# dt's softplus on GpSimd, with its transpose, sums and broadcast placed earlier in the first group

## The chip, the cores and the metric

The kernel runs on one core of a Trainium2 chip. The metric is the device time of one execution in microseconds (us). The core has five engines that work side by side, each through its own list of instructions in order: TensorE (PE: matrix products and transposes, results into eight PSUM banks), VectorE (DVE) and ScalarE (ACT) for elementwise work, GpSimd (POOL), and SyncE (SP), which here only issues DMA transfers. Engines wait for each other through semaphores; an instruction that waits holds up everything behind it on its engine.

## The reference

A two-layer decoder trunk on 256 tokens of width 2048: a Mamba-2 layer, then sliding-window attention, each followed by a squared-ReLU MLP. The change lies in the Mamba-2 layer, in what it does with the step width dt (64 heads):

```python
zxbcdt = h @ w_in
z, xbc, dt_raw = ...                     # 4096, 6144 and 64 columns
xbc = silu(causal_conv(xbc) + conv_b)    # gives xs, Bm, Cm
dt = softplus(dt_raw + dt_bias)
A = -exp(A_log)
# per chunk of 128 tokens
xdt = xs * dt
cs = cumsum(dt * A)
decay = exp(where(causal, cs_i - cs_j, -inf))
y_intra = (C B^T * decay) @ xdt
y_inter = (C @ state) * exp(cs)
new_state = ...  exp(cs_last - cs) ...
```

The first thing that needs the broadcast rows of cs is the decay matrix of head group 0.

## The kernel before

All weights are read once, in chunks of 512 KB (128 x 1024 floats), through a ring of four raw buffers. For each chunk ACT makes a rounded high part `whi` (L820) and DVE the remainder `wlo` (L1258), into rings of eight slots. PE multiplies both. The function `step()` on ACT and on DVE handles one chunk; the order of the steps among the other work is written out by hand on each engine.

The first layer's input product goes by eight head groups. A group takes **row tiles** (`row_tile`: 128 output columns of B, C or xs for 256 tokens, two chunks each, 16 products at L451 and 16 at L457) and then a **column block**, the z block (`column_block`: 512 columns of z, eight chunks of 12 products at L476 to L478). The first group has one row tile more, the third, whose last 64 columns are dt. So its order on PE is: B, C, dt, four xs tiles, z block. Chunks are numbered c0, c1, ... in the order in which PE uses them: the fourth row tile (the first of xs) is c6 and c7, the fifth c8 and c9, and the z block of the first group is c14 to c21.

The row tiles use PSUM banks 0 and 1 in turn. Of each xs, B or C tile, ACT copies the cross product out (`cross`, L895), DVE adds it and frees the bank (`conv_sum`, L1381), makes the convolution (`conv`, L1391, L1395 twice, L1398), ACT the tanh (L905), DVE the silu product (L1403). The scan of group g is done in group g+1: PE transposes xs (`s1`), ACT makes the decay matrices of both chunks (`decay`, L922 and L926) from `csb`, the broadcast of the rows of cs, and DVE and PE go on from there.

What becomes of dt, step by step, with its engine:

- DVE adds the dt tile (`dt_add`, L1326) to `dth`; PE turns it into token order (`dt_transposes`, L528, bank 5).
- DVE adds the bias (L1334) and makes -|v| (L1339); ACT takes the exponential u (`dt_exp`, L875); DVE takes log(1+u) as a series in s = u/(u+2) (`softplus`, L1341 to L1361: the sum, the reciprocal, and 13 more), and writes `dt` and -dt*exp(A_log), `dv[11]`.
- PE sums `dv[11]` over the tokens by a triangular matrix (`dt_sums`, L571, L575, banks 4 and 5); DVE copies the result to `cs` (L1367); ACT takes two exponentials (`dt_decays`, L879, L881).
- PE turns cs (`cs_transposes`, L582); ACT copies it out (`dt_cs2`, L885, L887); POOL writes it to memory (L1997), copies the group's columns (L1962) and reads the rows back as a broadcast to all partitions, 1 MB, `csb` (L1963).

## Time and profile before

| | |
|---|---|
| median of 3 runs | 2385.54 us (2384.42 to 2387.88) |
| span of the profiled execution, first to last instruction | 2384.6 us |
| PE busy | 2368.3 us, 99% of the span |
| DVE busy | 1576.7 us, 66% |
| ACT busy | 1168.9 us, 49% |
| POOL busy | 42.7 us, 2% |
| chain that ended last | PE 94%, DVE 2%, DMA 1%, ACT 1%, issue 1% |

The profiled execution is known by its span; it lies 0.94 us below the median, inside the runs shown. PE busy at 99% says that only work added to PE, idle time of PE, or a lower clock of PE can move the end. The chain of work that ended last says where PE was not the one that everything waited for.

### The profile page before, as it was taken

The page shows a single profiled execution, that of the slowest core. Times are in us where ns is not written, and L with a number is a line of the kernel's source. Part 1 is how long each engine was busy: PE and PEld are TensorE (multiplying, and loading weights), DVE is VectorE, ACT ScalarE, POOL GpSimd, SP SyncE. Part 2 cuts the span into 40 slices and gives each one's busy share as a digit, 9 for nine tenths or more (in the row PEclk, how much of TensorE's full clock was granted, in tenths as well). Part 3 has the DMA queues.
Part 4 walks back from the last instruction along what each step waited for, and adds up shares of the span by engine and source line. Part 5 has one row for each costly group of instructions (what it writes and reads, how often), then busy time and mean ns, then how long its engine had stood idle before and what let it go on. Part 6 is the DMA issues. An engine that isn't in the chain of part 4 may idle for free.

```text
span 2384.6 us, 32345 instructions
## 1 busy us (share of the span) xinstructions
PE 2368.3 (99%) x12610; PEld 2001.0 (84%) x12610; DVE 1576.7 (66%) x2151; ACT 1168.9 (49%) x1742; POOL 42.7 (2%) x85
## 2 busy tenths in 40 slices
PE   9999999999999999999999999999999999999998
PEld 8888888888888888888888888778888888888886
DVE  7888888886568556556556577776864654655655
ACT  5555555564355444444345355774543443443441
POOL 0000000000000000000000000000000000000000
PEclk9999999999999999999999999999999999999999
DMA  8766666657657666666666646346776666666663
GB/s 234 222 198 191 191 188 192 193 163 243 193 181 229 218 187 188 198 186 193 195 187 188 200 157 204 117 132 200 200 234 187 190 196 183 194 199 187 191 195 109
DMA packets 487829, 455.10 MB, mean 191 GB/s; under 512 B 13792, under 2 KB 360080, under 8 KB 485392
## 3 DMA queue, kind: packets, MB, share of 16 engines
q1 hardware_dynamic: 484608, 433.51, 61.1%
q0 software_dynamic: 3088, 19.79, 2.4%
q8 instruction: 88, 1.44, 0.2%
q14 instruction: 45, 0.37, 0.0%
HBM read 450.55 MB, written 2.16 MB: 190 GB/s over the span
## 4 chain that ended last, share of the span: by engine, by line
PE 94%; DVE 2%; DMA 1%; ACT 1%; issue 1%; POOL 0%; SPq 0%; DVEq 0%; ACTq 0%
PE ps L451 25%; PE ps L476 16%; PE ps L477 15%; PE ps L478 15%; PE ps L457 13%; PE ps L509 2%; PE ps L507 2%; PE ps L508 2%; PE ps L528 1%; DVE wlo L1258 1%; PE ps L600 1%; ACT whi L820 0%; ACT pb L1178 0%; PE ps L714 0%; DMA csb<-cs_rows 0%
## 5 line engine op out<-in xcount | busy, mean ns | idle before, releaser
L1258 DVE TENSOR_TENSOR wlo<-raw,whi 128x1024 fp32r<-128x1024 f32 x817 | 994.9, 1223 | 678.2 <-ACT whi L820 677.3
L820 ACT ACTIVATE whi<-raw 128x1024 fp32r<-128x1024 f32 x817 | 860.0, 1057 | 848.8 <-PE ps L478 457.3
L451 PE MATMUL ps<-actA,whi 128*128 128x512 f32 x2704 | 650.0, 392 | 2.8 <-DVE xpad L1381 2.3
L451 PEld LDWEIGHTS ps<-actA,whi 128*128 128x128 f32 x2704 | 498.2, 189 | 101.4 <-DVE xpad L1381 2.5
L476 PE MATMUL ps<-whi,actB 128*128 128x512 f32 x1056 | 412.8, 391 | 0.0
L477 PE MATMUL ps<-wlo,actB 128*128 128x512 f32 x1056 | 411.0, 389 | 0.0
L478 PE MATMUL ps<-whi,actB 128*128 128x512 f32 x1056 | 410.9, 389 | 0.0
L457 PEld LDWEIGHTS ps<-actA,wlo 128*128 128x128 f32 x2704 | 347.2, 191 | 13.5
L457 PE MATMUL ps<-actA,wlo 128*128 128x256 f32 x2704 | 351.3, 283 | 0.0
L476 PEld LDWEIGHTS ps<-whi,actB 128*128 128x128 f32 x1056 | 198.2, 188 | 42.9 <-issue 1.3
L478 PEld LDWEIGHTS ps<-whi,actB 128*128 128x128 f32 x1056 | 198.2, 188 | 41.4
L477 PEld LDWEIGHTS ps<-wlo,actB 128*128 128x128 f32 x1056 | 198.3, 188 | 40.3
L476 PE MATMUL ps<-whi,actA 128*128 128x512 f32 x544 | 215.9, 397 | 0.0
L477 PE MATMUL ps<-wlo,actA 128*128 128x512 f32 x544 | 212.0, 390 | 0.0
L478 PE MATMUL ps<-whi,actA 128*128 128x512 f32 x544 | 212.0, 390 | 0.0
L476 PEld LDWEIGHTS ps<-whi,actA 128*128 128x128 f32 x544 | 102.2, 188 | 22.5 <-issue 1.3
L478 PEld LDWEIGHTS ps<-whi,actA 128*128 128x128 f32 x544 | 102.1, 188 | 21.6
L477 PEld LDWEIGHTS ps<-wlo,actA 128*128 128x128 f32 x544 | 102.3, 188 | 19.7
L834 ACT ACTIVATE actB<-fsq 128x256 fp32r<-128x256 f32 x120 | 50.2, 419 | 110.6 <-DVE fsq L1740 110.6
L1589 DVE TENSOR_TENSOR res<-ps,res 128x512 f32<-128x512 f32 x80 | 51.9, 686 | 62.6 <-PE ps L509 32.6
L905 ACT ACTIVATE thb<-xh 128x256 f32<-128x256 f32 x48 | 19.8, 413 | 115.2 <-DVE xh L1398 115.2
L1740 DVE SCALAR_TENSOR_TENSOR fsq<-fb 128x256 f32<-128x256 f32 x120 | 51.0, 425 | 4.1
(209 smaller groups left out, 1683.9 us busy)
## 6 DMA issues: line engine op xcount, KB each, us to landing
raw<-in_mlp_w SPq DMA_DIRECT2D x512, 512.0 KB, 4.5
raw<-in_a_w_in SPq DMA_DIRECT2D x162, 512.0 KB, 4.5
raw<-in_a_w_out SPq DMA_DIRECT2D x64, 512.0 KB, 4.7
raw<-in_b_w_q SPq DMA_DIRECT2D x32, 512.0 KB, 4.9
raw<-in_b_w_o SPq DMA_DIRECT2D x32, 512.0 KB, 4.0
csb<-cs_rows POOLq DMA_DIRECT2D x8, 1024.0 KB, 7.1
raw<-in_kv_w SPq DMA_DIRECT2D x16, 512.0 KB, 4.2
gb<-in_ln_g POOLq DMA_DIRECT2D x4, 1024.0 KB, 7.0
```

The lines of the kernel that those rows point to most:

```text
L451: e.matmul(ps[:, b, :], whi[:, s, k * P:(k + 1) * P], act[:, kt, :, :].rearrange("p a n -> p (a n)"), start=(kt == 0), stop=False)
L457: last = e.matmul(ps[:, b, T:2 * T], wlo[:, slots[half], k * P:(k + 1) * P], act[:, kt, 0, :], start=False, stop=(kt == KT - 1))
L476: e.matmul(ps[:, b0 + h, :], act[:, kt, 0, tk], whi[:, s, w], start=(kt == 0), stop=False)
L477: e.matmul(ps[:, b0 + h, :], act[:, kt, 0, tk], wlo[:, s, w], start=False, stop=False)
L478: last = e.matmul(ps[:, b0 + h, :], act[:, kt, 1, tk], whi[:, s, w], start=False, stop=(kt == KT - 1))
L507: e.matmul(ps[:, b0 + h, :], act[:, kt, 0, tk], hi_w, start=(kt == 0), stop=False)
L508: e.matmul(ps[:, b0 + h, :], act[:, kt, 0, tk], lo_w, start=False, stop=False)
L820: e.activation(whi[:, s, :], raw[:, r, :], ACT.Copy).then_inc(w_hi_done, C.up(w_hi_done))
L834: e.activation(dst, src, ACT.Copy).then_inc(act_hi_done, C.up(act_hi_done))
L1258: e.tensor_tensor(wlo[:, s, :], raw[:, r, :], whi[:, s, :].bitcast(F32), ALU.subtract).then_inc(w_split, C.up(w_split))
L1589: ins = e.tensor_tensor(r, ps[:, b, :], r, ALU.add)
L1740: e.scalar_tensor_tensor(fsq[:, i % 2, :], fb[:, i % 2, :], 0.0, fb[:, i % 2, :], ALU.max, ALU.mult).then_inc(f_squared, C.up(f_squared))
```

## The change

The diff, without the renamed arithmetic that stays the same:

```diff
@@ tensor, first_group
                 for i in range(4):
                     row_tile(i % 2, actA, lo_last=i > 0)
-                column_block(2, actA, after={0: [dt_transposes], 4: [dt_sums], 6: [cs_transposes]})
+                    if i == 0:
+                        dt_transposes()
+                column_block(2, actA, after={0: [dt_sums], 2: [cs_transposes]})
@@ scalar, first_group
                 constants_out()
                 cross(3, 10)
+                dt_exp()
                 step()
...
-                dt_exp()
-                for _ in range(4):
-                    step()
                 C.n[full[4]] += 1
                 dt_decays()
                 step()
-                step()
-                step()
                 dt_cs2()
-                step()
+                for _ in range(7):
+                    step()
@@ vector
-            def softplus():
+            def dt_in():
...
+            def dt_reciprocal():
                 e.wait_ge(uexp_ready, C.next(uexp_ready))
                 e.tensor_scalar(den_, u, 2.0, None, ALU.add).then_inc(dve_step, C.up(dve_step))
                 e.wait_ge(dve_step, C.now(dve_step))
-                e.reciprocal(rec, den_).then_inc(dve_step, C.up(dve_step))
...
+                e.reciprocal(rec, den_).then_inc(rec_ready, C.up(rec_ready))
@@ vector, first_group
                 conv(2, 0)
                 step()
                 step()
+                dt_in()
                 silu(2, 0)
                 conv(3, 0)
+                dt_reciprocal()
                 step()
                 step()
...
                 silu(5, 0)
-                step()
-                step()
-                softplus()
-                step()
-                step()
                 dt_sums()
+                step()
+                step()
                 rotations_out()
-                for _ in range(6):
+                for _ in range(8):
                     step()
@@ gpsimd
+            def softplus():
+                e.wait_ge(rec_ready, C.next(rec_ready))
+                e.tensor_tensor(s_, u, rec, ALU.mult).then_inc(pool_step, C.up(pool_step))
+                e.wait_ge(pool_step, C.now(pool_step))
+                e.tensor_tensor(s2_, s_, s_, ALU.mult).then_inc(pool_step, C.up(pool_step))
+                e.wait_ge(pool_step, C.now(pool_step))
+                e.tensor_scalar(q_, s2_, 1.0 / 15, None, ALU.mult).then_inc(pool_step, C.up(pool_step))
+                e.wait_ge(pool_step, C.now(pool_step))
+                for k in (13, 11, 9, 7, 5, 3):
+                    e.tensor_scalar(q_, q_, 1.0 / k, None, ALU.add).then_inc(pool_step, C.up(pool_step))
+                    e.wait_ge(pool_step, C.now(pool_step))
+                    e.tensor_tensor(q_, q_, s2_, ALU.mult).then_inc(pool_step, C.up(pool_step))
+                    e.wait_ge(pool_step, C.now(pool_step))
+                e.tensor_scalar(v, v, 0.0, None, ALU.max)
+                e.tensor_scalar(q_, q_, 1.0, 2.0, ALU.add, ALU.mult).then_inc(pool_step, C.up(pool_step))
+                e.wait_ge(pool_step, C.now(pool_step))
+                e.tensor_tensor(lp, q_, s_, ALU.mult).then_inc(pool_step, C.up(pool_step))
+                e.wait_ge(pool_step, C.now(pool_step))
+                dtf = dt[:, :, :].rearrange("p c h -> p (c h)")
+                e.tensor_tensor(dtf, v, lp, ALU.add).then_inc(pool_step, C.up(pool_step))
+                e.wait_ge(pool_step, C.now(pool_step))
+                e.tensor_scalar(q_, dtf, -1.0, None, ALU.mult).then_inc(pool_step, C.up(pool_step))
+                e.wait_ge(pool_step, C.now(pool_step))
+                e.tensor_tensor(dv[:, 11, :].rearrange("p (c h) -> p c h", c=NH), q_.rearrange("p (c h) -> p c h", c=NH),
+                                eA[:, :].unsqueeze(1).broadcast_to([P, NH, NHD]), ALU.mult).then_inc(dt_ready, C.up(dt_ready))
@@ gpsimd, main line
             for x, value in ((mhalf, -0.5), (per_gw, 1.0 / GW), (epsilon, EPS)):
                 e.memset(x, value)
+            softplus()
             e.wait_ge(cs_turned, C.next(cs_turned))
```

`dt_in` holds the bias and -|v|, as before. On GpSimd the fused two-step operations are split, so 13 operations of VectorE become 21 of GpSimd, each but one followed by a wait for the one before it. The counts of `step()` on each engine stay the same in sum.

On PE, where the first chunk of the first z block (c14) ends, the order before has dt's transposes:

```order
L478 MATMUL ps<-whi,actA 128x512
L528 MATMUL ps<-ident,dth 128x128 x2
L476 MATMUL ps<-whi,actA 128x512
L477 MATMUL ps<-wlo,actA 128x512
L478 MATMUL ps<-whi,actA 128x512
```

and the order after has the sums there (L571 and L575 of before are L572 and L576):

```order
L479 MATMUL ps<-whi,actA 128x512
L572 MATMUL ps<-dv,kst 128x64 x2
L576 MATMUL ps<-dv,kst 128x64
L477 MATMUL ps<-whi,actA 128x512
L478 MATMUL ps<-wlo,actA 128x512
```

The sums moved forward by four chunks of the z block, the transposes of dt out of it, behind the fourth row tile.

On DVE, from the convolution of the fifth row tile (the second of xs) to the products that remain before the cs copy, the order before has all of dt's arithmetic in one piece, behind the last silu and two chunks:

```order
L1403 SCALAR_TENSOR_TENSOR xT<-thb,xh 128x256
L1258 TENSOR_TENSOR wlo<-raw,whi 128x1024 x2
L1334 TENSOR_TENSOR dv<-ps,dtb 128x128
L1339 SCALAR_TENSOR_TENSOR dv<-dv 128x128
L1341 TENSOR_SCALAR dv<-dv 128x128
L1343 RECIPROCAL dv<-dv 128x128
...
L1361 SCALAR_TENSOR_TENSOR dv<-dt,eA 128x128
L1258 TENSOR_TENSOR wlo<-raw,whi 128x1024 x2
L1367 COPY cs<-ps 128x128
```

and the order after has its first four operations around the convolution of the fifth row tile:

```order
L1258 TENSOR_TENSOR wlo<-raw,whi 128x1024 x2
L1334 TENSOR_TENSOR dv<-ps,dtb 128x128
L1339 SCALAR_TENSOR_TENSOR dv<-dv 128x128
L1385 SCALAR_TENSOR_TENSOR xT<-thb,xh 128x256
L1363 TENSOR_TENSOR xpad<-ps,xpad 128x256
L1373 TENSOR_SCALAR xh<-xpad,cwg 128x256
L1377 SCALAR_TENSOR_TENSOR xh<-xpad,cwg,xh 128x256 x2
L1380 SCALAR_TENSOR_TENSOR xh<-xpad,cwg,xh 128x256
L1343 TENSOR_SCALAR dv<-dv 128x128
L1345 RECIPROCAL dv<-dv 128x128
L1258 TENSOR_TENSOR wlo<-raw,whi 128x1024 x2
```

Two operations moved ahead of that convolution and two behind it; the other 13 left DVE.

On POOL, behind the constants that it sets at the start, before:

```order
L1992 DMA Dsk<-in_a_D 128x64
L1995 MEMSET small 128x2 x3
L1997 DMA cs_rows<-cst 64x256
L1962 COPY csg<-cs 128x16
L1963 DMA csb<-cs_rows 128x2048
```

and after, where `dv` is dt's work space:

```order
L2003 MEMSET small 128x2 x3
L1967 ISA
L1967 TENSOR_TENSOR dv<-dv 128x128
L1969 TENSOR_TENSOR dv<-dv 128x128
L1971 TENSOR_SCALAR dv<-dv 128x128
...
L1986 TENSOR_SCALAR dv<-dt 128x128
L1988 TENSOR_TENSOR dv<-dv,eA 128x128
L2006 DMA cs_rows<-cst 64x256
```

The 21 operations stand ahead of the write of cs and of everything else that POOL does later.

## Rows read from the trace of the kernel before

**Rows 1.** Chain that ended last, 60 to 98 us: start us, us, what.
```profile
70.93 5.50 DMA raw<-in_a_w_in
...
77.58 0.28 ACT cst L885
...
82.55 8.51 DMA csb<-cs_rows
```

**Rows 2.** Timeline of PE, second group: start, us, engine, line, operation, [idle before <-releaser].
```profile
89.53 3.82 PE L451 MATMUL ps<-actA,whi 128*128 128x512 f32 x16
...
97.53 5.53 PE L451 MATMUL ps<-actA,whi 128*128 128x512 f32 x16 [2.28 <-DVE xpad L1381]
```

**Rows 3.** Timeline of PE, the same two row tiles of the third group.
```profile
154.36 3.82 PE L451 MATMUL ps<-actA,whi 128*128 128x512 f32 x16
...
159.93 3.82 PE L451 MATMUL ps<-actA,whi 128*128 128x512 f32 x16
```

**Rows 4.** Timeline of ACT, third group: its first decay.
```profile
148.67 2.45 ACT L922 ACTIVATE em<-csb,csg 128x128 f32<-128x128 f32 x8
```

**Rows 5.** Stretches: us, busy PE, PEld, DVE, ACT, POOL, PEclk, DMA share, GB/s.
```profile
97.50:100.00 2.50, 2.47 (x8) 1.95 (x9) 2.38 (x6) 2.47 (x6) 0.93 (x2) 0.69 0.62 171
...
102.00:103.00 1.00, 1.00 (x6) 0.82 (x5) 1.00 (x2) 1.00 (x2) 0.00 (x0) 1.00 1.01 385
```

**Rows 6.** Timeline of PE, first group: fifth row tile; dt's transposes, sums, cs transposes.
```profile
37.17 3.82 PE L451 MATMUL ps<-actA,whi 128*128 128x512 f32 x16
...
56.62 0.38 PE L528 MATMUL ps<-ident,dth 128*128 128x128 f32 x2
...
67.77 0.55 PE L571 MATMUL ps<-dv,kst 128*128 128x64 f32 x4
...
73.93 0.38 PE L582 MATMUL ps<-ident,cs 128*64 128x128 f32 x2
```

**Rows 7.** Timeline of DVE, first group, 33 to 63 us.
```profile
33.89 0.42 DVE L1326 TENSOR_TENSOR dth<-ps,dth 128x256 f32<-128x256 f32 x1
...
42.80 0.42 DVE L1403 SCALAR_TENSOR_TENSOR xT<-thb,xh 128x256 f32<-128x256 f32 x1
...
45.71 1.22 DVE L1258 TENSOR_TENSOR wlo<-raw,whi 128x1024 fp32r<-128x1024 f32 x1
...
51.28 1.22 DVE L1258 TENSOR_TENSOR wlo<-raw,whi 128x1024 fp32r<-128x1024 f32 x1
52.80 1.23 DVE L1258 TENSOR_TENSOR wlo<-raw,whi 128x1024 fp32r<-128x1024 f32 x1 [0.30 <-ACT whi L820]
...
61.89 0.95 DVE L1343 RECIPROCAL dv<-dv 128x128 f32<-128x128 f32 x1
62.88 0.29 DVE L1345 TENSOR_TENSOR dv<-dv 128x128 f32<-128x128 f32 x1
```

**Rows 8.** Timeline of POOL.
```profile
82.41 0.20 POOL L1962 COPY csg<-cs 128x16 f32<-128x16 f32 x1 [3.48 <-DMA cs_rows<-cst]
...
157.41 0.47 POOL L1962 COPY csg<-cs 128x16 f32<-128x16 f32 x1 [27.21 <-ACT em L922]
...
676.93 0.19 POOL L1977 TENSOR_TENSOR small<-small 128x1 f32<-128x1 f32 x1 [139.84 <-DVE small L1645]
677.19 0.57 POOL L1980 TENSOR_TENSOR small<-small 128x1 f32<-128x1 f32 x1
690.32 0.70 POOL L1977 TENSOR_TENSOR small<-small 128x1 f32<-128x1 f32 x1 [12.55 <-DVE small L1645]
691.09 1.43 POOL L1980 TENSOR_TENSOR small<-small 128x1 f32<-128x1 f32 x1
```

**Rows 9.** Timeline of DVE beside three of those operations.
```profile
156.82 1.01 DVE L1395 SCALAR_TENSOR_TENSOR xh<-xpad,cwg,xh 128x256 f32<-128x256 f32 x2
...
690.27 0.69 DVE L1270 TENSOR_TENSOR actA<-hf_early,actA 128x512 fp32r<-128x512 f32 x1
690.88 1.22 DVE L1258 TENSOR_TENSOR wlo<-raw,whi 128x1024 fp32r<-128x1024 f32 x1
```

More of the change, by code:

```diff
@@ L142, in build @@
     clamped = nc.alloc_semaphore("clamped")
+    rec_ready = nc.alloc_semaphore("rec_ready")
     nab_ready = nc.alloc_semaphore("nab_ready")
@@ L1328, in dt_add @@
                 e.memset(small[:, 95:96], 0.0).then_inc(dt_summed, C.up(dt_summed))
-            v, nab, u, den_, rec, s_, s2_, q_, lp = [dv[:, i, :] for i in range(9)]
-            def softplus():
+            v, nab, u, den_, rec = [dv[:, i, :] for i in range(5)]
+            def dt_in():
                 e.wait_ge(per_head_in, C.next(per_head_in, 3))
@@ L1501, in first_group @@
                 silu(5, 0)
+                dt_sums()
                 step()
                 step()
-                softplus()
-                step()
-                step()
-                dt_sums()
                 rotations_out()
-                for _ in range(6):
+                for _ in range(8):
                     step()
@@ L1981, in norm_rstd @@
                         rstd_ready, C.up(rstd_ready))
+            v, _, u, _, rec, s_, s2_, q_, lp = [dv[:, i, :] for i in range(9)]
+            def softplus():
[23 more added lines that the diff above has]
+                                eA[:, :].unsqueeze(1).broadcast_to([P, NH, NHD]), ALU.mult).then_inc(dt_ready, C.up(dt_ready))
             e.wait_ge(x_in[2], C.next(x_in[2]))
```

20 lines of the change are left out of this document (removed).

## The prediction, made before the changed kernel ran

> **What bounds the kernel now.** I read the page first: PE is busy for 99% of the span and 94% of the chain that ended last. So I looked for the places where that chain is not PE, and there is one of size behind the start: from 60 to 98 us it runs through dt. Its steps are the arithmetic of softplus, a load of weights (5.50 us from 70.93), ACT's copy of cs at 77.58, and the broadcast `csb`, 8.51 us from 82.55 [rows 1]. Behind it ACT makes the first decay and only then the weight chunk that DVE and PE want, and PE's fourth row tile of the second group starts 8.00 us after the third, with 2.28 us idle, released by DVE's convolution sum [rows 2]. In the third group the same two tiles are 5.57 us apart [rows 3].
>
> **What that place is worth.** The idle time with its restart costs 8.00 - 5.57 = 2.43 us. The 16 products behind it take 5.53 us, not 3.82: 1.71 more [rows 2, 3]. The stretches say why: the granted clock is 0.69 in the mean from 97.5 to 100, so part of it at 1.2 GHz, after PE had been idle, and full again (2.4 GHz) from 102 [rows 5]. Together 4.1 us, 0.17% of the span. If everything else were free, the change could bring this and no more, since no other wait hangs on dt.
>
> Does the new order remove it? Call T the time at which PE makes the sums. Before, T is 67.77, `csb` lands at 91.06, 23.3 later [rows 6, 1]. In that, ACT copied cs out 3.65 us after PE's transposes at 73.93 because chunks of weights stood ahead of the copy in ACT's order and one waited for its load [rows 6, 1]. The new order has one chunk between the exponentials and the copy, and the transposes still two chunks behind the sums: about 20 us from T to landing. In the third group, where nothing is late, the first decay starts 5.7 us ahead of the third tile [rows 3, 4]; for the second group that is 83.8. With T at 56.62 `csb` lands near 77, with a margin of 7 us, and when PE is held up at the sums both ends move with it. So the old wait goes, whatever else happens: -4.1.
>
> **The moved pieces, one by one.** dt's transposes on PE, now ahead of the fifth row tile at 37.17 [rows 6]: their input is ready at 34.5, 0.2 after `dt_add` ends at 34.31 [rows 7]. No wait; they cost PE the same 0.3 us here as there. `dt_in` on DVE goes between 42.80 and the silu: two operations of about 0.3 us, of which 0.2 falls into idle time ahead of the sum; the convolution ends 0.45 us later. ACT's exponential (0.3 us) is ready long before it is needed. The sum and the reciprocal stand behind the convolution: 45.71 + 0.45 + 0.26 + 0.95 = 47.4 for the end of the reciprocal [rows 7]. DVE and ACT now run about 1.2 to 1.6 us later through the last tiles. PE does not notice: c13, which DVE then finishes near 48.5 instead of 46.9, is used from 50.1, and each later chunk has more slack, 4 us and more in the z block. Chunks c18 and later now wait on DVE behind the copy of cs, which waits for the sums; PE takes c18 9 us after the sums, and DVE needs 2 us for it. No cost. The 13 operations that leave DVE (some 4.6 us from 62.88) were hidden; they bring nothing.
>
> **The piece that decides: 21 operations on POOL, and PE waits for the last.** PE reaches the sums after c14, at 56.62 [rows 6]. Until then POOL has 56.6 - 47.5 = 9.1 us, 0.43 us for each of 21. The trace shows no POOL operation of this shape. From below: one of 128x1 takes 0.19 us, and the next starts 0.26 after it; a copy of 16 columns takes 0.20 [rows 8]. At 0.26 the chain would take 5.5 us and PE would not wait. From above, undisturbed: DVE takes 0.29 for 128x128 [rows 7]; with the 0.07 for the semaphore 0.36, and twice DVE's time would be 0.65. I take 0.45, the floor of 0.26 with 0.15 to 0.2 for the 127 columns more: 9.5 us, ready at 57.0, a wait of 0.5.
>
> But POOL is not undisturbed. The same copy takes 0.20 us at 82.41 and 0.47 at 157.41, where it ends at 157.88, 0.05 after a DVE operation of two inputs from SBUF (157.34 to 157.83) [rows 8, 9]. The addition of one column takes 0.19 at 676.93 and 0.70 at 690.32: it ends at 691.02, and DVE's two-input subtraction beside it at 690.96. The next one takes 1.43 instead of 0.57: DVE's subtraction of 128x1024 ended at 692.10 [rows 8, 9]. So a POOL operation that starts while DVE reads two inputs from SBUF is held until that instruction ends, and then gets its turn. From 47.4 on DVE does little else: subtractions of 1.13 us, silu, three steps of each convolution. The Trainium skill, "SBUF — State Buffer", section "Who interferes with whom", says it as a rule: a VectorE instruction with two SBUF inputs and a GpSimd one that reads SBUF exclude each other for the whole instruction. By that rule too, the trace agrees (0.19 against 0.70).
>
> Counted in turns, with one POOL operation after each two-input DVE instruction and two in the 0.9 us of a sum and a one-input multiply between them: two subtractions and silu, 3 done by 50; the window, 5 by 51; three convolution steps, 8 by 52.6; subtractions of c15 and c16 and silu, 11 by 55.4; window, 13 by 56.4; convolution, 16 by 58; c17 and silu, 18 by 59.2. Then DVE itself stands at the cs copy, and the last 3 take 0.43 each: 60.5. DVE in turn is held by the POOL operations, some 0.07 us for each of 16: 61.6. PE waits from 56.6 to 61.6: **+5.0**. For the columns at nothing this count gives 59.3, +2.7; with 0.27 us and 0.2 us more for two and one input, 64.0, +7.4.
>
> The Trainium skill, "GPSIMD Engine Reference", section "3.1 Elementwise — side-by-side cycle accounting", gives 4497 ns for a two-input add of 2048 columns. An estimate from that page is 0.28 us for 128 columns, the upper end of what I counted; the wait would be about 6 us by it.
>
> After a wait of 2.28 us PE lost 1.71 to the clock [rows 2, 5]; I take +1.7 again, more for a longer wait being unseen.
>
> **Sum.** -4.1 + 5.0 + 1.7 = +2.6 us. Against the profiled span 2384.6 that is 2387.2; against the median of the runs, 0.94 higher, **2388.1**. With the ends of the wait, 2.7 and 7.4, it is +0.3 to +5.0, so 2385.8 to 2390.5. A measurement of this kernel can tell about 0.2%, 4.8 us: most of this counts as no change.
>
> **Rival A: POOL is fast enough.** The holding up costs little, because it applies to few instants or because POOL slips in between dependent DVE steps, and the chain takes its undisturbed 5.5 to 10 us. Then PE waits 0 to 1 us with no loss of clock, and the gain stays: -4.1 to -3.0, 2381.4 to 2382.5, still within 0.2%. For it: only tiny POOL operations were seen. Against it: each of the shown ones that met a two-input DVE instruction was held to its end. Chance 0.2.
>
> **Rival B: slower.** The same hold, but POOL loses the turn to a DVE instruction that is already queued, and advances only while DVE has no two-input one: in each row tile's 5.57 us the 0.9 us window and the 0.3 before the second subtraction [rows 7], 3 operations or so. Then 7 are done when DVE stops at the cs copy near 59, and 14 x 0.43 = 6.0 remain: ready at 65.0, PE waits 8.4, and with the clock and the gain +6.0: 2391.5. It decides from a wait of 7.2 us on, dt ready after 63.8. For it: several subtractions started 0.08 before the one ahead ended; against it: the addition at 690.32 did get its turn between two of them [rows 8, 9]. POOL operations dearer by 0.15 us than I took end here too. Chance 0.21.
>
> **Rival C: a first use costs.** POOL has not run a one-input multiply or add before this point, and a first use could cost time that the trace does not show; its first copy took the least of all, 0.20 [rows 8]. Each microsecond of it lengthens PE's wait by one; from 2.2 on the kernel is slower by over 0.2%, and with 3 (about seven undisturbed operations of 0.43) it would take 2391. The Trainium skill, "GPSIMD Engine Reference", "2.1 Instruction dispatch", gives some 6 us for the first call of a freshly loaded function, by which it would be 2394; no row here shows one. Chance 0.04.
>
> **Rival D: the change does not do what it says,** because `csb` stays last, through slower small transfers beside the weight loads. The margin of 7 us speaks against it. 2392. Chance 0.02.
>
> **How the numbers follow.** Forecast 0.53, rival A 0.2, B 0.21, C 0.04, D 0.02. Faster by more than 0.2% needs 4.8 us, over the 4.1 that are there: 0.03, out of A, for what I may have missed. Slower: B, C, D less what falls short of the bound, plus the end of the forecast: 0.28. The rest, 0.69, within. The range reaches from A's 2381.3 to B with a little more, 2392.5.
>
> **What the new profile would show.** PE: the 2.28 us ahead of the fourth row tile of the second group gone and its 16 products at 3.8 us; a new wait ahead of the sums in the first z block, released by POOL, of 3 to 7 us, and products behind it at a lower granted clock. POOL: 21 operations from 47.5 to about 61.5, some of 0.3 to 0.5 us and those beside DVE's subtractions of 1 us and more. DVE: idle ahead of the cs copy. `csb` on chip some 7 us before its use. I am wrong if POOL's operations don't end with DVE's two-input ones, if the chain takes under 9 us or over 17, or if PE waits elsewhere.

## The result, and the profile after

| | before | after |
|---|---|---|
| median, 10 runs each | 2385.54 us (2384.34 to 2389.33) | 2392.39 us (2391.92 to 2393.25) |
| ratio to before | | 1.0029 (95% interval 1.0021 to 1.0037) |
| span of the profiled execution | 2384.6 us | 2390.3 us |

The kernel is 0.29% slower. The forecast was 2388.1 with a range of 2381.3 to 2392.5: the time lies inside it, at its upper end, and outside the 0.2% that the forecast called no change. The spans differ by 5.7 us and the medians by 6.9; the readings below explain the 5.7.

**Where the time goes, in one table.** Two points of PE's timeline cut the stretch that the change touches: the start of the transposes of xs in the second group and the same in the third. In the profile they are the lines "ident,xT ... x8".

```profile
92.35 1.04 PE L529 MATMUL ps<-ident,xT 128*128 128x128 f32 x8
```

| start of that line | before | after | difference |
|---|---|---|---|
| second group | 82.44 | 92.35 | +9.91 |
| third group | 147.24 | 153.02 | +5.78 |
| between them | 64.80 | 60.67 | -4.13 |

So the first group lost 9.9 us, the second gave 4.13 back, and behind the third group's mark nothing more changes (5.78 against 5.7 in the spans). What the loss is made of, the list of PE's waits of after says (wait: us in total, times, longest):

```profile
PE ps L572 <- POOL dv L1988: 7.3, 1, 7.3
```

and PE's timeline, with the transposes of dt, the sums, and the third and fourth row tiles of the second group, which answer to [rows 2] (L452 is L451 of before, L572 is L571):

```profile
37.13 0.38 PE L529 MATMUL ps<-ident,dth 128*128 128x128 f32 x2
...
64.24 1.11 PE L572 MATMUL ps<-dv,kst 128*128 128x64 f32 x4 [7.26 <-POOL dv L1988]
...
99.46 3.82 PE L452 MATMUL ps<-actA,whi 128*128 128x512 f32 x16
...
105.02 3.82 PE L452 MATMUL ps<-actA,whi 128*128 128x512 f32 x16
```

PE waits 7.26 us at the sums. The old 2.28 us ahead of the fourth row tile of the second group are gone (the two tiles start 5.56 us apart, not 8.00), and its 16 products take 3.82 us instead of 5.53. The remaining 9.91 - 7.26 = 2.65 us is the clock. The stretches of after show it (columns as in [rows 5]: length, busy PE, PEld, DVE, ACT, POOL, granted clock, DMA share, GB/s):

```profile
56.00:60.00 4.00, 0.98 (x5) 0.48 (x3) 3.86 (x7) 1.65 (x3) 3.57 (x6) 0.90 0.70 224
60.00:64.00 4.00, 0.00 (x0) 0.00 (x0) 0.04 (x1) 0.66 (x1) 3.43 (x8) 0.50 0.44 131
64.00:68.00 4.00, 3.76 (x12) 3.28 (x13) 2.57 (x5) 1.31 (x3) 0.18 (x1) 0.50 0.02 4
68.00:72.00 4.00, 4.00 (x16) 3.21 (x15) 1.42 (x4) 0.00 (x0) 0.00 (x0) 0.82 0.93 253
```

The clock falls to 0.50 (1.2 GHz) while PE stands idle, and PE works on at that level until some way into the last stretch: 3.76 x 0.50 + 4.00 x 0.18 = 2.6 us of full-speed work lost. A mean of 0.82 over 4.00 us is 0.36 of them at 0.50, so PE works at the lower level for 3.76 + 1.44 = 5.2 us. Note the last columns too: from 64 to 68 us hardly any data moves (4 GB/s). That comes up again below.

**POOL**, the new chain, from its first to its last operation:

```profile
47.26 1.31 POOL L1967 TENSOR_TENSOR dv<-dv 128x128 f32<-128x128 f32 x1 [31.58 <-DVE dv L1345]
48.64 1.26 POOL L1969 TENSOR_TENSOR dv<-dv 128x128 f32<-128x128 f32 x1
49.99 0.59 POOL L1971 TENSOR_SCALAR dv<-dv 128x128 f32<-128x128 f32 x1
...
52.67 1.50 POOL L1976 TENSOR_TENSOR dv<-dv 128x128 f32<-128x128 f32 x1
54.26 1.50 POOL L1974 TENSOR_SCALAR dv<-dv 128x128 f32<-128x128 f32 x1
55.85 0.47 POOL L1976 TENSOR_TENSOR dv<-dv 128x128 f32<-128x128 f32 x1
56.40 0.58 POOL L1974 TENSOR_SCALAR dv<-dv 128x128 f32<-128x128 f32 x1
57.06 0.46 POOL L1976 TENSOR_TENSOR dv<-dv 128x128 f32<-128x128 f32 x1
...
58.27 1.50 POOL L1976 TENSOR_TENSOR dv<-dv 128x128 f32<-128x128 f32 x1
...
63.73 0.46 POOL L1988 TENSOR_TENSOR dv<-dv,eA 128x128 f32<-128x128 f32 x1
```

and DVE beside it:

```profile
47.09 2.56 DVE L1258 TENSOR_TENSOR wlo<-raw,whi 128x1024 fp32r<-128x1024 f32 x2
...
51.00 1.20 DVE L1377 SCALAR_TENSOR_TENSOR xh<-xpad,cwg,xh 128x256 f32<-128x256 f32 x2
...
52.63 1.22 DVE L1258 TENSOR_TENSOR wlo<-raw,whi 128x1024 fp32r<-128x1024 f32 x1
54.15 1.23 DVE L1258 TENSOR_TENSOR wlo<-raw,whi 128x1024 fp32r<-128x1024 f32 x1 [0.29 <-ACT whi L823]
...
58.23 1.22 DVE L1258 TENSOR_TENSOR wlo<-raw,whi 128x1024 fp32r<-128x1024 f32 x1
```

The chain runs from 47.26 to 64.19, 16.9 us. Five operations take 1.26 to 1.50 us, and each lies beside one of DVE's 128x1024 subtractions, ending some 0.3 us behind it (52.63 + 1.22 = 53.85, POOL 54.17). Of the other sixteen, fourteen take 0.45 to 0.47 (two inputs) and 0.53 to 0.59 (one input), beside DVE's 128x256 steps too (57.06, beside the convolution at 56.6 to 57.8). The two left are a one-input operation at 50.66, beside such steps, with 0.71 us, and the one at 61.65, which does not wait for the one ahead of it, with 0.30. From one start to the next these are about 0.55 and 0.66 us.

### The profile page after: what moved, and what is told of

It reads as the page before. It is cut to its first block, busy times and chain, and to the rows that moved or that the text cites. A ratio compares the mean times of both kernels' runs of the same rounds, so it can differ in the third digit from the quotient of the medians.

```text
span 2390.3 us, 32353 instructions
## 1 busy us (share of the span) xinstructions
PE 2368.6 (99%) x12610; PEld 2001.2 (84%) x12610; DVE 1573.1 (66%) x2138; ACT 1168.5 (49%) x1742; POOL 58.5 (2%) x106
## 3 DMA queue, kind: packets, MB, share of 16 engines
q8 instruction: 88, 1.44, 0.2%
## 4 chain that ended last, share of the span: by engine, by line
PE 95%; DVE 2%; ACT 1%; POOL 1%; issue 1%; DMA 0%; SPq 0%; DVEq 0%; ACTq 0%
PE ps L452 25%; PE ps L477 16%; PE ps L478 16%; PE ps L479 16%; PE ps L458 13%; PE ps L510 2%; PE ps L508 2%; PE ps L509 2%; PE ps L529 1%; PE ps L601 1%; ACT whi L823 0%; ACT pb L1178 0%; DVE wlo L1258 0%; DMA xin<-in_x 0%; PE ps L717 0%
## 5 line engine op out<-in xcount | busy, mean ns | idle before, releaser
L452 PE MATMUL ps<-actA,whi 128*128 128x512 f32 x2704 | 648.3, 391 | 0.5 <-DVE wlo L1258 0.5
L452 PEld LDWEIGHTS ps<-actA,whi 128*128 128x128 f32 x2704 | 497.2, 188 | 98.1 <-issue 0.7
L477 PEld LDWEIGHTS ps<-whi,actA 128*128 128x128 f32 x544 | 102.7, 189 | 22.7 <-issue 1.3
```

The lines of the kernel that those rows point to most:

```text
L452: e.matmul(ps[:, b, :], whi[:, s, k * P:(k + 1) * P], act[:, kt, :, :].rearrange("p a n -> p (a n)"), start=(kt == 0), stop=False)
L477: e.matmul(ps[:, b0 + h, :], act[:, kt, 0, tk], whi[:, s, w], start=(kt == 0), stop=False)
```

## The experiments

Nine kernels ran. Each comparison with before is a ratio to the runs of before in the same series, with its 95% interval. One table serves all: the marks are the ones of the table above, "waits" are PE's idle time at the sums and ahead of row tiles of the second group.

| kernel | median us | ratio (interval) | span | second group mark | third group mark | between | waits: sums; second group |
|---|---|---|---|---|---|---|---|
| before | 2385.54 | | 2384.6 | 82.44 | 147.24 | 64.80 | 0; 2.28 |
| after | 2392.39 | 1.0029 (1.0021, 1.0037) | 2390.3 | 92.35 | 153.02 | 60.67 | 7.26; 0 |
| one_sbuf_input | 2386.69 | 1.0005 (0.9996, 1.0014) | 2384.9 | 86.93 | 147.59 | 60.66 | 2.75; 0 |
| sums_two_chunks_later | 2390.28 | 1.0020 (1.0011, 1.0029) | 2387.1 | 85.03 | 149.91 | 64.88 | 1.84; 2.37 |
| sums_three_chunks_later | 2389.13 | 1.0017 (1.0007, 1.0026) | 2386.6 | 83.42 | 149.39 | 65.97 | 0.62; 3.44 |
| before_cs_copy_ahead | 2386.38 | 1.0004 (0.9995, 1.0013) | 2386.6 | 83.24 | 149.31 | 66.07 | 0; 3.57 |
| quarter_broadcast | 2387.14 | 1.0002 (0.9993, 1.0011) | 2385.3 | 83.23 | 148.15 | 64.92 | 0.66; 2.79, 0.55, 0.29 |
| four_chunks_ahead_of_cs_copy | 2386.02 | 1.0001 (0.9992, 1.0010) | 2384.0 | 83.76 | 146.76 | 63.00 | 0.77; 0.85, 0.56, 0.32 |
| softplus_spread_on_dve | 2385.47 | 0.9999 (0.9990, 1.0008) | 2383.7 | 82.72 | 146.44 | 63.72 | 0; 0.62, 1.50, 0.32 |
| no_stand_gpsimd | 2386.11 | 1.0003 (0.9994, 1.0012) | 2386.5 | 86.53 | 149.23 | 62.70 | 2.12; 0.55, 0.57, 0.27 |
| no_stand_dve | 2384.95 | 0.9996 (0.9987, 1.0005) | 2382.9 | 82.43 | 145.64 | 63.21 | 0; 1.04, 0.58, 0.30 |

The third group's mark follows the span within 0.2 us in every row, so it shows where in an execution the time goes. It is not a finer measure of a kernel than the median: span and marks are those of one execution, while the runs of before alone reach from 2384.34 to 2389.33, and its median moved by a microsecond from series to series (2385.41, 2386.24 and 2385.98 in the three behind this table). The executions of before_cs_copy_ahead and no_stand_gpsimd that are read here lie 2.0 and 2.2 us above their kernels' medians, those of sums_two_chunks_later and sums_three_chunks_later 1.4 and 0.7 us below. Part of a mark is also settled before any edit is reached: PE starts the fifth row tile at 37.17 us in before, 37.26 in after, 37.42 in sums_three_chunks_later, 37.81 in sums_two_chunks_later and 37.97 in before_cs_copy_ahead. So a difference of a microsecond between two marks shows nothing by itself; the waits inside one execution, and what released them, do.

### Is POOL held by DVE's instructions? (one_sbuf_input)

The theory: a POOL operation stands while DVE reads both inputs from SBUF. The rival: POOL is that slow by itself beside a busy DVE. The experiment leaves the order of after as it is and gives the subtractions of c13 to c17 one input from PSUM, with the same shape. What DVE writes for these five chunks is therefore not the remainder of the weights.

```diff
-                    e.tensor_tensor(wlo[:, s, :], raw[:, r, :], whi[:, s, :].bitcast(F32), ALU.subtract).then_inc(
+                    other = whi[:, s, :].bitcast(F32) if not one_input[0] else ps[:, 6:8, :].rearrange("p b n -> p (b n)")
+                    e.tensor_tensor(wlo[:, s, :], raw[:, r, :], other, ALU.subtract).then_inc(
```

> The changed kernel, but for chunks c13 to c17 DVE subtracts PSUM banks 6 and 7 (same width, same length of instruction) instead of the high part, so that those five instructions read one input from SBUF; those chunks' low parts are so not the right ones. My theory: these five instructions hold up five of GpSimd's 21 operations by 4.6 us in sum (1.26 to 1.50 us each, against 0.46 to 0.59); without that GpSimd is done near 59.7, PE waits 2.6 to 3 us instead of 7.3, the clock costs about 1.7, and the time is near 2386 to 2387. Rival: GpSimd's long operations are not held by DVE's second input; then they stay at 1.3 to 1.5 us, PE waits 7.3 us, and the time is 2392.

POOL's timeline in this kernel, first, two of the middle and the last:

```profile
47.17 0.45 POOL L1971 TENSOR_TENSOR dv<-dv 128x128 f32<-128x128 f32 x1 [31.56 <-DVE dv L1347]
...
53.23 0.46 POOL L1980 TENSOR_TENSOR dv<-dv 128x128 f32<-128x128 f32 x1
53.78 0.53 POOL L1978 TENSOR_SCALAR dv<-dv 128x128 f32<-128x128 f32 x1
...
59.13 0.46 POOL L1992 TENSOR_TENSOR dv<-dv,eA 128x128 f32<-128x128 f32 x1
```

and two of DVE's subtractions beside it, as long as before (the one at 53.55 lies over POOL's 53.78):

```profile
47.00 2.29 DVE L1260 TENSOR_TENSOR wlo<-raw,ps 128x1024 fp32r<-128x1024 f32 x2
...
53.55 1.22 DVE L1260 TENSOR_TENSOR wlo<-raw,ps 128x1024 fp32r<-128x1024 f32 x1 [0.30 <-ACT whi L823]
```

No operation of POOL is above 0.64 us any more, and the chain takes 47.17 to 59.59, 12.4 us. PE's wait is 2.75 instead of 7.26, the median 5.7 us lower. The Trainium skill, "SBUF — State Buffer", section "Who interferes with whom", calls it an exclusive lock between a VectorE instruction with two SBUF inputs and a GpSimd one that reads SBUF; by that rule, this trace agrees for the 128x1024 subtraction (1.50 us against 0.46 and 0.53). Beside the two-input steps of 128x256 POOL shows at most 0.71 us for an operation of some 0.56; there DVE is the one that takes longer, 0.51 to 0.68 us for each of the three silu products beside the chain, where [rows 7] has 0.42. Two parts of PE's wait now have a size: 2.75 us is POOL's own slowness, 4.51 us is being held.

### Does the sums' place alone decide? (sums_two_chunks_later, sums_three_chunks_later)

If the loss is only PE's arrival ahead of dt, sums placed later should cost nothing and the 4.1 us of the old wait should remain as a gain. The first of the two:

```diff
-                column_block(2, actA, after={0: [dt_sums], 2: [cs_transposes]})
+                column_block(2, actA, after={2: [dt_sums], 4: [cs_transposes]})
```

> The changed kernel, with PE's two places moved alone: the sums behind c16 and cs's transposes behind c18. My theory: what the change costs is PE's wait of 7.3 us for GpSimd's last operation (ready at 64.2), with the clock behind it; PE now comes to the sums at 62.4, waits 1.8 us, and loses at most 1.7 to the clock. The old wait of the second group (4.2 us) stays away. So 2383 to 2385, against 2392.4 for the changed kernel and 2385.5 for the kernel before. Rival 1: GpSimd's work costs by something else than that wait (DVE held up, its later chunks); then most of the 7 us stays, 2389 or more. Rival 2: without the early sums the broadcast is late again; then 2387 or more, with a wait ahead of the fourth row tile of the second group.

and the second, in which DVE also subtracts two chunks, and ACT splits one more, ahead of their copies of cs:

```diff
-                column_block(2, actA, after={0: [dt_sums], 2: [cs_transposes]})
+                column_block(2, actA, after={3: [dt_sums], 5: [cs_transposes]})
@@ scalar, first_group
                 dt_decays()
                 step()
+                step()
                 dt_cs2()
-                for _ in range(7):
+                for _ in range(6):
                     step()
@@ vector, first_group
-                dt_sums()
                 step()
                 step()
+                dt_sums()
                 rotations_out()
```

> The changed kernel with PE's sums behind c17 and cs's transposes behind c19, DVE's copy of cs behind c18 and c19 instead of ahead of them, and ACT's copy one chunk later. My theory: PE reaches the sums at 65.2, a microsecond after GpSimd is done, so no wait there; the broadcast lands near 86 to 87, which ACT wants at 84, and PE has 4 us more of slack; no wait, no loss of clock: 2385.5 - 4.2 = 2381.3. Rival 1 (cost elsewhere than the wait): 2388 or more. Rival 2 (the broadcast becomes late): a wait ahead of the fourth row tile of the second group, 2383 to 2386.

The first half held: the wait at the sums fell to 1.84 and 0.62 us, with no loss of clock, and the first group was late by 2.6 and 1.0 us instead of 9.9, of which 0.64 and 0.25 were there at the fifth row tile already. The second half did not: the second group has a wait again, and one row tile earlier than in [rows 2], ahead of its third. This is rival 2 in kind, a wait in the second group, though not by a late broadcast. PE's timeline, first of sums_two_chunks_later, then of sums_three_chunks_later:

```profile
94.66 5.50 PE L452 MATMUL ps<-actA,whi 128*128 128x512 f32 x16 [2.37 <-DVE xpad L1363]
```

```profile
94.11 5.54 PE L452 MATMUL ps<-actA,whi 128*128 128x512 f32 x16 [3.44 <-DVE xpad L1364]
```

`csb` is not what is late. In sums_three_chunks_later ACT reaches the decay without idle time, and what it waited for ahead of it is a load of weights. Its timeline, with the copy of cs at its head:

```profile
72.59 0.38 ACT L888 ACTIVATE cst<-ps 64x256 f32<-64x256 f32 x1 [3.26 <-PE ps L583]
...
85.28 1.06 ACT L823 ACTIVATE whi<-raw 128x1024 fp32r<-128x1024 f32 x1 [4.63 <-DMA raw<-in_a_w_in]
...
93.22 2.14 ACT L925 ACTIVATE em<-csb,csg 128x128 f32<-128x128 f32 x7
```

The chain that ended last holds that load (start, length, what), and the stretches of the same kernel show what went before it:

```profile
77.71 9.30 DMA raw<-in_a_w_in
```

```profile
68.00:72.00 4.00, 4.00 (x20) 3.29 (x19) 2.36 (x2) 1.33 (x2) 0.00 (x0) 1.00 0.24 59
72.00:76.00 4.00, 4.00 (x20) 3.25 (x19) 1.82 (x2) 3.38 (x6) 0.62 (x1) 1.00 0.75 219
```

From 68 to 72 us, before had 175 GB/s; here it is 59, because ACT stands 3.26 us for PE's transposes of cs and splits nothing, so no raw buffer comes free and no load goes out. When ACT goes on, it splits four chunks in a row, their buffers come free close together, and the load that goes out at 77.71 takes 9.30 us. A new theory follows: an engine of the split that stands for dt uses up the lead of the loads. What the runs of these two kernels lose beyond the executions read here, 1.4 and 0.7 us in the medians, no profile shows.

### Is an early csb enough without POOL's softplus? (before_cs_copy_ahead)

Before, with one edit: ACT copies cs out one chunk behind the exponentials, as after does, not three. Everything else of dt stays where it was.

```diff
                 dt_decays()
                 step()
-                step()
-                step()
                 dt_cs2()
+                step()
+                step()
                 step()
```

> The kernel before, with ACT's copy of the turned cs put two weight chunks earlier and nothing else. My theory: the broadcast was late by 4.2 us for ACT and 2.3 us for PE because ACT made that copy at 77.6, 3.7 us after PE's transposes, behind chunks that waited for their loads. With the copy at 74.4 the broadcast lands near 88, ACT waits about 1 us, PE not at all: 2385.5 - 4.1 = 2381.4 without any work on GpSimd. Rival: the place of softplus is what makes the broadcast late and the copy is not; then 2384 to 2385.5.

`csb` goes out only 0.84 us earlier (81.71 against 82.55 [rows 1]), and in this execution PE waits longer, not shorter, in the second group, ahead of the fourth row tile; the third group starts 2.1 us later. Of that, 0.80 us was there at the fifth row tile of the first group, ahead of the edit. PE's timeline, with that tile at its head, and, from the chain that ended last, the load that ACT waited for:

```profile
37.97 3.82 PE L451 MATMUL ps<-actA,whi 128*128 128x512 f32 x16
...
99.62 5.51 PE L451 MATMUL ps<-actA,whi 128*128 128x512 f32 x16 [3.57 <-DVE xpad L1381]
```

```profile
81.74 10.40 DMA raw<-in_a_w_in
```

A load of weights is late here too, in an order that has no softplus on POOL. It went out 0.03 us behind the 1 MB of `csb`. Whether that or the traffic of the loads themselves made it 10.40 us long, this kernel alone doesn't say; the next one asks it. In the medians the edit changes nothing (1.0004, interval 0.9995 to 1.0013): shown is that the gain of 4.1 us stays out, not that the edit costs time.

### Is it the broadcast that slows the load? (quarter_broadcast)

sums_three_chunks_later, with the first group's broadcast cut from eight heads to two, 256 KB; the decay matrices of that group are made from those two heads alone.

```diff
+                heads = GH if g else GH // 4
-                e.dma_start(csb[:, :, :].rearrange("p h n -> p (h n)"),
-                            cs_rows[g * GH:(g + 1) * GH, :].rearrange("(a h) n -> a (h n)", a=1).broadcast_to([P, GH * T])
+                e.dma_start(csb[:, 0:heads, :].rearrange("p h n -> p (h n)"),
+                            cs_rows[g * GH:g * GH + heads, :].rearrange("(a h) n -> a (h n)", a=1).broadcast_to([P, heads * T])
```

> The kernel of sums_three_chunks_later, but the first group's broadcast brings 2 of the 8 heads' rows (256 KB on chip, not 1 MB), and the decays of that group read these two for all eight; the first group's decays are so not the right ones. Theory: the broadcast takes engine time from the weight loads beside it; with a quarter of it the slow load takes 6 us or less, PE's wait at the third row tile falls from 3.4 to under 1 us, and 3 to 5 us go. Rival: the loads are late only because they were issued late, by ACT's stand at the copy; then the load still lands at about the same time and 3 us of wait stay.

The chain that ended last and PE's timeline:

```profile
77.52 8.63 DMA raw<-in_a_w_in
```

```profile
93.26 3.94 PE L452 MATMUL ps<-actA,whi 128*128 128x512 f32 x16 [2.79 <-DVE xpad L1367]
```

With three quarters of the broadcast gone the load is 0.67 us shorter and the wait 0.65 us. So in the load's length the broadcast has a share, and it is the small one; the load stays long without it. The theory's 6 us or less, with a wait under 1 us, did not come. In the time the share is not small: this wait of 2.79 us cost no clock (3.94 us for the products, where 3.44 us of idle had cost 5.54), which gives back 1.6 us, of which two new waits (0.55 and 0.29 us) take half. The third group's mark moved by 1.24 us in all, the median, from another series, by 2.0.

### A longer row of chunks ahead of the stand (four_chunks_ahead_of_cs_copy)

sums_three_chunks_later with four chunks instead of two between ACT's exponentials and its copy of cs:

```diff
                 dt_decays()
-                step()
+                for _ in range(4):
+                    step()
                 dt_cs2()
-                for _ in range(7):
+                for _ in range(4):
                     step()
```

> The kernel of sums_three_chunks_later, but ACT splits four weight chunks (c20 to c23) between its exponentials and its copy of cs, not two. Theory now: while ACT stands at that copy for PE's transposes of cs, no weights are split, so no raw buffer comes free and no load is issued (59 GB/s from 68 to 72 us); the loads behind it then run beside the 1 MB broadcast, one of them takes 9.3 us instead of 4.5, and PE waits 3.4 us at the third row tile of the second group, with 1.7 of clock. With four chunks ahead ACT is busy in that time, the loads go out 3 to 5 us earlier, the wait goes, and the span is near 2381.5 instead of 2386.6, the runs some 5 us below those of sums_three_chunks_later. Rival: the broadcast alone slows the loads, whatever lead there is; then the wait of 3 us stays, 2386 or more.

ACT's timeline and the load in the chain that ended last:

```profile
72.93 0.38 ACT L888 ACTIVATE cst<-ps 64x256 f32<-64x256 f32 x1 [1.38 <-PE ps L583]
```

```profile
78.76 7.93 DMA raw<-in_a_w_in
```

The stand is 1.38 us instead of 3.26, the core moves 209 GB/s from 60 to 80 us instead of 177, and the second group takes 63.00 us instead of 65.97; the medians, of different series, are 3.1 us apart (2386.02, 2389.13). The two kernels differ in nothing but two chunks of ACT's order, so this is the shown part of the theory, at some three fifths of the 5 us expected. Whether it is the shorter stand or the two chunks that ACT is further ahead, the edit does not separate. Over before there is no gain that can be told: 0.5 us at the third mark, a ratio of 1.0001.

### Softplus on DVE, in pieces (softplus_spread_on_dve)

The same order, with POOL out of it: 13 operations on DVE, in pieces behind the silu of the last three tiles.

```diff
+            def series(ks):
+                for k in ks:
+                    e.scalar_tensor_tensor(q_, q_, 1.0 / k, s2_, ALU.add, ALU.mult).then_inc(dve_step, C.up(dve_step))
+                    e.wait_ge(dve_step, C.now(dve_step))
...
+                dt_start()
...
+                series((13, 11, 9, 7))
...
+                series((5, 3))
+                dt_end()
+                dt_sums()
```

> The kernel of four_chunks_ahead_of_cs_copy, but the softplus stays on DVE, as in the kernel before (13 operations of 0.30 us), in three pieces: behind the silu of the fifth, the sixth and the seventh row tile. Theory: DVE falls 5 to 6 us behind but PE's chunks are 5 us and more ahead in the z block; dt is ready near 63, two microseconds ahead of PE's sums at 65.2, no wait at the sums (0.6 on GpSimd): the same time as four_chunks_ahead_of_cs_copy or 0.6 us less. Rival: DVE has no room there; PE then waits for c15 or c17 in the z block, 2 us or more, and GpSimd was worth its price.

PE waits neither at the sums nor elsewhere in the z block, and neither the third mark (0.3 us ahead) nor the median (0.55 us lower) tells this version from the one with POOL. What POOL took over was cheap on DVE once it was spread.

### Two more chunks ahead of what waits for the sums (no_stand_gpsimd, no_stand_dve)

Both engines now split the last two chunks of the z block, c20 and c21, ahead of what waits for the sums; the first kernel has softplus on POOL, the second on DVE as above.

```diff
@@ scalar, first_group
+                for _ in range(2):
+                    step()
                 dt_decays()
-                step()
+                for _ in range(2):
+                    step()
                 dt_cs2()
@@ vector, first_group
                 silu(5, 0)
+                for _ in range(4):
+                    step()
                 dt_sums()
```

> The kernel of four_chunks_ahead_of_cs_copy, with two more chunks (c20, c21) split ahead of ACT's exponentials and ahead of DVE's copy of cs. Theory: what is left of PE's waits in the second group (1.7 us, in three pieces) comes from DVE and ACT standing for the sums (DVE 4 us, ACT 6 us) while raw buffers are full and no load goes out. With two chunks more ahead of the stand, the loads go out then, the second group takes 61 us instead of 63.0, and the span falls from 2384.0 to about 2382. Rival: the loads cannot go faster around there anyway (the copy to memory, the broadcast and the weights share the engines); then the second group keeps 63 us and the span stays at 2384.

> The kernel of softplus_spread_on_dve with the same two chunks ahead of the two waits for the sums. Theory: the second group takes 61 to 62 us instead of 63.7, the span falls from 2383.7 to about 2381.5 to 2382.5; the runs about 2 us under those of softplus_spread_on_dve. Rival: DVE is the engine that is full here, so the later copy of cs makes the broadcast late and ACT waits for it; span 2384 or more.

In spite of the names, ACT still stands in both: 3.99 us at the exponentials and 4.81 at the copy of cs in no_stand_gpsimd, 2.02 us and nothing in no_stand_dve. On POOL the edit works against itself: DVE's further subtractions hold the chain that DVE and PE wait for. POOL's timeline in no_stand_gpsimd, and PE's wait:

```profile
64.88 1.34 POOL L1987 TENSOR_TENSOR dt<-dv 128x128 f32<-128x128 f32 x1
...
66.92 0.45 POOL L1991 TENSOR_TENSOR dv<-dv,eA 128x128 f32<-128x128 f32 x1
```

```profile
PE ps L572 <- POOL dv L1991: 2.1, 1, 2.1
```

On DVE it gives the best third mark of all, 145.64, 1.6 us ahead of before; the span is 1.7 lower. Its median, 2384.95, has a ratio of 0.9996 (0.9987 to 1.0005): no gain that can be told. The second group still takes 63.21 us instead of 60.67, with three waits that add up to 1.92, and ACT still waits 4.03 us for a load there, though of the stands for the sums and for cs only 2.02 us are left (ahead of them ACT stood 4.06 us for DVE's convolution):

```profile
85.63 1.06 ACT L823 ACTIVATE whi<-raw 128x1024 fp32r<-128x1024 f32 x1 [4.03 <-DMA raw<-in_a_w_in]
```

## Why the prediction came out as it did, step by step

**The place of the cost: right.** PE waits ahead of the sums, released by POOL's last operation, with a lower clock behind. POOL's chain took 16.9 us, just inside the 9 and 17 named as bounds, and its long operations lie beside DVE's two-input subtractions.

**The hold: right in kind and size, not in form.** The count of turns gave 57.0 to 61.6, 4.6 us; with one_sbuf_input, 4.5 were measured. But the count put one POOL operation behind each two-input instruction of DVE, the 128x256 steps of the convolution too. The trace shows five long holds beside 128x1024 subtractions, with 1.26 to 1.50 us for an operation of about 0.5, and next to none beside the short ones. Two differences cancelled, fewer holds and each longer; that the sizes agree is luck.

**The price of a POOL operation: too low.** This is the term that made the wait 7.26 and not 5.0. I took 0.45 us from start to start; it is about 0.55 with two inputs and 0.66 with one, and the chain that no 128x1024 two-input instruction disturbs takes 12.4 us, not 9.5. So even without any hold PE would wait 2.75 us, where the prediction had 0.5. Twice DVE's time, the upper end that [rows 7] gave (0.65), was the better row than the tiny operations of [rows 8]. The prediction's own end for dearer operations (dt ready at 64.0, a wait of 7.4) is what was measured (64.19, 7.26), though how it gets from 61.6 to 64.0 it does not work out. The figure of GpSimd's two-input add that the Trainium skill gives ("GPSIMD Engine Reference", "3.1 Elementwise — side-by-side cycle accounting") scaled, as an estimate, to a wait of about 6 us and was nearer than my forecast.

**The clock: +1.7 predicted, +2.65 measured.** The prediction said that a longer wait had not been seen. 7.26 us of idle left PE at the lower level for 5.2 us of work. The range of the forecast itself ended at +5.0, with the wait at 7.4 and the clock at 1.7; it is the clock that carries the sum past it.

**The old wait: right for this order, too wide as a statement.** Its working on `csb` holds: the broadcast, sent at 77.33, takes 7.7 to 8.2 us, so lands near 85, 20.8 behind the sums (20 predicted), and its first use is at 96.06: the margin is 11 us. After shows -4.13, one_sbuf_input -4.14. But in four other orders with `csb` no longer last, PE waited 2.4 to 3.6 us again, for loads, and the prediction had looked at no load. Such a late load is in after and in one_sbuf_input too. ACT's timeline of after, then of one_sbuf_input:

```profile
73.36 0.38 ACT L888 ACTIVATE cst<-ps 64x256 f32<-64x256 f32 x1 [6.21 <-PE ps L583]
...
86.19 1.06 ACT L823 ACTIVATE whi<-raw 128x1024 fp32r<-128x1024 f32 x1 [4.73 <-DMA raw<-in_a_w_in]
```

```profile
67.94 0.38 ACT L888 ACTIVATE cst<-ps 64x256 f32<-64x256 f32 x1 [5.84 <-PE ps L583]
...
80.70 1.06 ACT L823 ACTIVATE whi<-raw 128x1024 fp32r<-128x1024 f32 x1 [4.60 <-DMA raw<-in_a_w_in]
```

Why did PE not wait there? Count from ACT's copy of cs to ACT's restart behind the late load, to the sum on DVE that frees the bank of the second group's third row tile, and to the time at which PE comes to that tile (its start less its wait):

| us behind ACT's copy of cs | late load in | DVE's sum starts | PE comes | PE waits |
|---|---|---|---|---|
| after (copy at 73.36) | 12.8 | 23.0 | 26.1 | 0 |
| one_sbuf_input (67.94) | 12.8 | 22.9 | 26.1 | 0 |
| sums_two_chunks_later (71.48) | 12.6 | 22.7 | 20.8 | 2.37 |
| sums_three_chunks_later (72.59) | 12.7 | 21.1 | 18.1 | 3.44 |

The late load keeps its distance from the copy. What changes is PE's: with the sums behind c14 it comes 3 us after DVE's sum has started, with the sums two or three chunks later it comes first. The time that PE loses at the sums doesn't enter, for the copy waits for PE's transposes behind the sums and moves with it: after lost 9.9 us there and one_sbuf_input 4.5, and both have 26.1. So "both ends move" was the right reason, for the loads as well as for `csb`, and it was luck that the margin was there for the loads, which the prediction had not asked for. "Whatever else happens" goes too far: the -4.1 belongs to the early place of the sums, and each kernel that moved them later gave half of it or more back (62.70 to 65.97 us between the marks, against 60.67). before_cs_copy_ahead, with its wait at the fourth tile, is outside this table; what makes the load late in all of them, the stand, the broadcast or the traffic as a whole, is shown only in the parts above.

So my sum was -4.1 + 5.0 + 1.7 = +2.6; measured is -4.13 + 7.26 + 2.65 = +5.78. Whether the gain of 4.1 can be had stays open. It takes dt ready by 57 us with the sums still behind c14, and no kernel here had both: POOL undisturbed is done at 59.6, and the version on DVE has the sums behind c17. Such a version would, by this sum, reach 2381.4; the lowest median here is 2384.95, of no_stand_dve.

**The number.** The forecast's own ends were 2385.8 and 2390.5, and 2392.39 lies above them, in the part of the range that was kept for rival B. Of the 4.3 us between forecast and median, 3.2 are in the sum above; 1.1 are not, since the medians differ by 6.9 us and the spans by 5.7.

**The rivals.** Rival B is what the time looks like (2391.5, deciding from a wait of 7.2 us or dt ready after 63.8; measured 7.26 and 64.2), but not by its main mechanism: POOL did get its turns; it was its second cause, dearer operations, that brought it. Rival A falls with the hold. Of rival C, a first use that costs time, there is no trace: the first one-input operation takes 0.59 us, as the later ones. In one_sbuf_input the first of all takes 0.45. Rival D is out.

**The small steps.** dt's transposes at 37.13 wait for nothing. The reciprocal ends at 47.17 (47.4 predicted). DVE reaches the z block about 1.3 us later (its subtraction at 56.84 in before is at 58.23) and PE waits for no chunk. The stand of DVE at the copy of cs was called "no cost" as well; it cost no wait of PE in the z block, but ACT stands 5.2 us at the exponentials and 6.2 us at its own copy of cs, hardly any data moves from 64 to 68 us (4 GB/s), and a load is late behind it, unseen only because PE needs it 3 us later still. The prediction looked at who needs the chunks behind the stand, and not at who refills the buffers.

**Left open.** What the waits of 1.4 to 2.4 us in sum hang on that remain in the second group of the last four kernels: the stands that are left, the broadcast, or small transfers among the loads, was not tried. Nor was an order without any stand, nor softplus spread on DVE with the sums still behind c14.

## What to carry to other kernels

Where an engine in order both prepares chunks and frees the buffers of a load ring, a wait placed in its list costs twice: the chunks behind it, which one checks, and the loads that don't go out, which show only some 20 us later as a wait behind one long load (72.6 to 90.7 us in sums_three_chunks_later, 71.5 to 92.3 in sums_two_chunks_later). Before moving a chain of dependent small operations to POOL, price each from start to start with the number of inputs, add the rest of each large two-input DVE instruction that runs beside it, and ask whether the same operations, spread over DVE's list, are not already hidden. And a wait that is traced to one late input can have a second one behind it, as the load here behind `csb`: ask for the margin of each input at the place where it is used, and count it from the event that moves with it.

## What the runs showed of the hardware

- On POOL, with no 128x1024 two-input instruction of DVE beside it, 128x128 of float32 takes 0.53 to 0.59 us with one input and 0.45 to 0.47 with two (after): among operations that wait for the one before, the one with fewer inputs is the dearer. The one that does not wait took 0.30. Between dependent ones lie 0.06 to 0.09 us.
- A POOL operation beside a 128x1024 subtraction of DVE ends some 0.3 us behind it; beside 128x256 operations it is hardly held (0.71 us at most in after). DVE pays too: the pair of subtractions at 47.09 takes 2.56 us where an undisturbed pair has 2.36, and the pair of convolution steps at 51.00 takes 1.20, not 1.01 ([rows 9]).
- The same idle time of PE does not always cost the clock. The 16 products behind it took 5.50 to 5.54 us after 2.28, 2.37, 3.44 and 3.57 us, but 3.94 after 2.79 us in quarter_broadcast. At the sums, 1.84 us cost none (granted clock 1.00 from 64 to 68 us in sums_two_chunks_later), 2.12 us did (0.59 from 68 to 72 us in no_stand_gpsimd), and so did 2.75 us in one_sbuf_input (0.63 from 60 to 64 us). After waits of 0.55 to 1.50 us they took 3.92 to 3.96. What differs in quarter_broadcast, no run here shows.
- The load of 512 KB that PE ends up waiting for took 7.93 to 10.40 us (four_chunks_ahead_of_cs_copy, quarter_broadcast, sums_three_chunks_later, sums_two_chunks_later with 9.82, before_cs_copy_ahead), where the median load of this matrix takes 4.4 us in the whole execution of after.
